# Hyena core of a two-block network: a turn-over through four banks, and the last unit's products by halves of the channels

## The chip, the cores and the metric

The kernel runs on one core of a Trainium2 chip. The metric is the device time of one execution in microseconds (us), lower being better. The program is one long kernel: a first block (delta-rule and stick-breaking mixers, gated feed-forward), a second block with an attention layer, and a third with a Hyena long convolution. The change touches only the core of the Hyena mixer, some 236 us out of about 3,126.

## The reference, cut to what matters

```python
def hyena_mixer(h, w_in, conv_w, conv_b, f_w1, ..., f_freq, skip, w_out, z, decay):
    u = dwconv3(h @ w_in, conv_w, conv_b)
    v, x1, x2 = jnp.split(u, 3, axis=-1)
    a = jnp.sin(f_freq * (z @ f_w1 + f_b1))
    a = jnp.sin(f_freq * (a @ f_w2 + f_b2))
    filt = (a @ f_w3).reshape(L, HY_ORDER, 2, D) * decay[:, None, None, :]
    ...
    k2 = k2 / jnp.sum(jnp.abs(k2), axis=0, keepdims=True)
    kf = jnp.fft.rfft(k2, axis=0)
    gates = (x1, x2)
    zc = v
    for o in range(HY_ORDER):
        zf = jnp.fft.rfft(zc, n=2 * L, axis=1)
        y = jnp.fft.irfft(zf * kf[None, :, o], n=2 * L, axis=1)[:, :L]
        zc = gates[o] * (y + skip[o] * zc)
    return zc @ w_out
```

L is 512 positions, D is 1024 channels, HY_ORDER is 2. All is float32.

## The kernel before, in words

The core works in four units, `UNITS = 2 * ORDERS`. Unit u is one order (u // 2) and one half of the channels (512 of them, u % 2). The discrete transforms are matrix products with tables of cosines and sines, split by parity of the position, so that only half the frequencies are computed and the others come from sums and differences; `f` (0 or 1) is one tile of 128 frequencies.

The steps of a unit, with names and lines of the profile:

- Turn-over, `turn_in` (L1477, TensorE): the unit's values U lie with channels on the partitions; sixteen 128x128 transposes turn them so that positions lie there, one tile t of positions per PSUM bank. The banks are `4 + t % 2`: from the third tile on TensorE waits (semaphore `y_tc`) until ScalarE has copied the bank two tiles back to ZK (`turned_in`, L1946).
- `filters` (L1439) makes the filter's values for a later unit into banks 0 to 7, pairwise, and VectorE multiplies them by the decay into PM (L2500, L2501). `filter_norm` (L1446) sums absolute values; VectorE's reciprocal rn of it (L2518) raises `y_rn`.
- `k_transform` (L1492) transforms PM into banks 0 to 3; ScalarE copies them to KS in one instruction (L1952, `y_kc`), and GpSimd forms the four sums and differences KP (L949 to L952, `y_kp`).
- `z_transform` (L1507) transforms ZK into banks 4 to 7. ScalarE copies banks 4 and 6 to XZ (L1958); VectorE's `multiply` (from L2538) makes sums and differences with banks 5 and 7 (L2538 to L2542, then `y_x`), and then the products with KP in two parts of six instructions (L2550 to L2556); each part raises `y_cb`.
- GpSimd's `y_parts` makes YF out of the products YB, two instructions behind each part (L960, L961, then L963, L964, which raises `y_y`).
- `inverse` (L1527) transforms YF back, with U's channel tile c in a bank; for the last unit the even and the odd positions of a tile go to banks of their own, `(4 + c, LAST_ODD[c])`. VectorE's `gated` scales, adds the skip term and multiplies by the gate (L2573, L2575, `y_z`). For units 2 and 3 ScalarE (L1971) and VectorE (L2564, `z_lo`) split the result into ZH and ZL, the operands of the output product `hy_out` (L490 to L492).

Each engine's instructions stand in a fixed order, written by hand, and run in that order; semaphores tie the engines. TensorE's order around the change is: for unit u, transforms of Z of u and K of u + 1, then `turn_in(u + 1)`, then `filters(u + 2)` (or, at u = 2, `z_transform(3, 0)`), then `inverse(u)`. ScalarE does `k_out(u + 1, 1)`, the KS copy, and right behind it the four copies of the turn-over. GpSimd does `y_parts(u, 0)`, `k_parts(u + 1, 0)`, `y_parts(u, 1)`, `k_parts(u + 1, 1)`. In the last unit TensorE waits for `y_x` of the whole of `multiply(3, 1)` ahead of the inverse products, because these go to banks 4 to 7, which that step reads; it then does f = 0 for all tiles and f = 1 for all tiles. The first slab of `hy_out`'s weights is split by GpSimd behind the last YF; SyncE loads the second slab once the last inverse product is done.

## Time and profile before

| what | value |
|---|---|
| median of 3 runs | 3129.38 us (3121.71 to 3134.8) |
| the profiled execution, its own time | 3128.08 us |
| its span, first to last instruction | 3125.9 us |
| TensorE (PE) busy | 2925.0 us, 94% |
| VectorE (DVE) busy | 1364.6 us, 44% |
| GpSimd (POOL) busy | 1642.2 us, 53% |
| ScalarE (ACT) busy | 714.8 us, 23% |
| mean granted clock of TensorE | 0.963 of full speed |

The profile is of one execution. A busy share is a mean over the whole program; what a change in one stage is worth is read from that stage's own timeline, where the brackets behind an instruction say how long its engine stood idle before it and who released it. A float32 product appears as two records of TensorE. Two instructions that follow one another on VectorE overlap at their ends, so the distance between two starts is less than one duration.

### The profile page before, as it was taken

What the parts mean: (1) busy time and instruction counts of PE and PEld (TensorE: products, weight loads), DVE (VectorE), ACT (ScalarE), POOL (GpSimd) and SP (SyncE); (2) the same over time, 40 slices, a digit from 0 to 9 for tenths busy, and PEclk for the clock granted to TensorE, in tenths of its full rate; (3) what the DMA queues carried; (4) which work ended last, traced back from release to release, by engine and by line L of the source; (5) the groups of instructions that cost most, each with busy time, mean ns of one, the idle gap of its engine ahead of it and who ended that gap; (6) DMA issues with size and microseconds to landing.
All of it is one profiled execution on the core that took longest, in us unless ns stands there. A gap on an engine that the chain in (4) does not pass through costs nothing.

```text
span 3125.9 us, 38862 instructions
## 1 busy us (share of the span) xinstructions
PE 2925.0 (94%) x14667; PEld 2360.3 (76%) x14667; DVE 1364.6 (44%) x1901; ACT 714.8 (23%) x1077; POOL 1642.2 (53%) x1573
## 2 busy tenths in 40 slices
PE   7997989999998999999998999999989999899998
PEld 6886888878976878788885547888867555678886
DVE  5575566321144037533334663332056677543312
ACT  2274222253243000211002562111011222121100
POOL 5652223364504666566664115667657443666663
PEclk9997899999999999999999999999999999999999
DMA  3221000022201245555652002333222110223331
GB/s 107 81 66 37 1 0 0 27 81 68 81 15 41 94 159 178 166 184 188 196 174 94 14 27 68 94 94 109 93 86 81 58 34 1 81 81 96 104 99 64
DMA packets 291816, 259.65 MB, mean 83 GB/s; under 512 B 6474, under 2 KB 264119, under 8 KB 291437
## 3 DMA queue, kind: packets, MB, share of 16 engines
q1 hardware_dynamic: 287840, 248.53, 25.5%
q0 software_dynamic: 2416, 6.57, 0.7%
q10 hardware_dynamic: 1436, 2.96, 0.3%
q8 instruction: 70, 1.15, 0.2%
q14 instruction: 54, 0.43, 0.0%
HBM read 255.94 MB, written 2.10 MB: 83 GB/s over the span
## 4 chain that ended last, share of the span: by engine, by line
PE 78%; DVE 10%; issue 5%; DVEq 2%; ACT 2%; POOL 1%; DMA 1%; POOLq 0%; ACTq 0%; SPq 0%
PE ps L490 20%; PE ps L492 20%; PE ps L491 20%; DVE cv L2045 2%; PE ps L1145 2%; PE ps L1132 1%; PE ps L1151 1%; DVE HS L627 1%; PE ps L1527 1%; PE ps L1372 1%; PE ps L1507 1%; PE ps L1362 1%; PE ps L1352 1%; PE ps L1492 1%; PE ps L1439 1%
## 5 line engine op out<-in xcount | busy, mean ns | idle before, releaser
L694 POOL CAST spl<-raw 128x512 fp32r<-128x512 f32 (+1 forms) x352 | 247.4, 703 | 730.4 <-PE ps L492 570.8
L490 PE MATMUL ps<-HSH,spl 128*128 128x512 f32 x1344 | 540.1, 402 | 40.6 <-DVE HSL L620 19.5
L696 POOL TENSOR_TENSOR spl<-raw,spl 128x512 fp32r<-128x512 f32 (+1 forms) x352 | 500.6, 1422 | 60.1 <-issue 10.5
L491 PE MATMUL ps<-HSL,spl 128*128 128x512 f32 x1344 | 529.8, 394 | 0.0
L492 PE MATMUL ps<-HSH,spl 128*128 128x512 f32 x1344 | 529.7, 394 | 0.0
L700 POOL TENSOR_TENSOR spl<-raw,spl 128x512 fp32r<-128x512 f32 (+1 forms) x352 | 480.0, 1364 | 51.5 <-issue 1.3
L490 PE MATMUL ps<-HNH,spl 128*128 128x264 f32 (+1 forms) x1152 | 370.5, 322 | 28.3 <-DVE HNL L622 6.0
L491 PE MATMUL ps<-HNL,spl 128*128 128x264 f32 (+1 forms) x1152 | 361.0, 313 | 0.0
L492 PE MATMUL ps<-HNH,spl 128*128 128x264 f32 (+1 forms) x1152 | 360.1, 313 | 0.0
L490 PEld LDWEIGHTS ps<-HSH,spl 128*128 128x128 f32 x1344 | 256.2, 191 | 121.2 <-issue 44.6
L698 POOL CAST spl<-raw 128x512 fp32r<-128x512 f32 (+1 forms) x352 | 229.6, 652 | 211.3 <-PE ps L492 209.1
L492 PEld LDWEIGHTS ps<-HSH,spl 128*128 128x128 f32 x1344 | 256.3, 191 | 54.8
L491 PEld LDWEIGHTS ps<-HSL,spl 128*128 128x128 f32 x1344 | 257.1, 191 | 52.7 <-issue 2.2
L490 PEld LDWEIGHTS ps<-HNH,spl 128*128 128x128 f32 x1152 | 222.5, 193 | 46.8 <-issue 24.2
L491 PEld LDWEIGHTS ps<-HNL,spl 128*128 128x128 f32 x1152 | 222.6, 193 | 13.2 <-issue 1.7
L492 PEld LDWEIGHTS ps<-HNH,spl 128*128 128x128 f32 x1152 | 221.4, 192 | 11.3
L490 PE MATMUL ps<-AFH,spl 128*128 128x512 f32 x528 | 208.1, 394 | 0.0
L492 PE MATMUL ps<-AFH,spl 128*128 128x512 f32 x528 | 207.2, 392 | 0.0
L491 PE MATMUL ps<-AFL,spl 128*128 128x512 f32 x528 | 205.3, 389 | 0.0
L905 POOL TENSOR_TENSOR lm<-lp,masks 128x512 f32<-128x512 f32 x56 | 74.5, 1356 | 208.3 <-DVE lp L2166 165.4
L2338 DVE TENSOR_TENSOR ps<-SG,ps 128x512 f32<-128x512 f32 x66 | 45.9, 696 | 264.6 <-PE ps L492 264.6
L2327 DVE SCALAR_TENSOR_TENSOR H<-ps,mod,H 128x512 f32<-128x512 f32 x32 | 24.0, 751 | 279.7 <-PE ps L492 279.7
(426 smaller groups left out, 4726.3 us busy)
## 6 DMA issues: line engine op xcount, KB each, us to landing
adw<-in_ada_w SPq DMA_DIRECT2D x96, 512.0 KB, 5.3
raw<-in_w_in SPq DMA_DIRECT2D x44, 1024.0 KB, 5.1
raw<-in_ffn_w_up SPq DMA_DIRECT2D x88, 512.0 KB, 4.9
raw<-in_w_ffn_in SPq DMA_DIRECT2D x44, 512.0 KB, 5.1
raw<-in_ffn_w_down SPq DMA_DIRECT2D x16, 1408.0 KB, 6.1
raw<-in_hy_w_in SPq DMA_DIRECT2D x12, 1024.0 KB, 5.1
raw<-in_w_ffn_out SPq DMA_DIRECT2D x8, 1408.0 KB, 7.0
raw<-in_w_branch_dn SPq DMA_DIRECT2D x8, 1024.0 KB, 5.1
```

Source lines behind the costliest of these rows:

```text
L490: pe.matmul(dst, w[0], x[0], start=first, stop=False)
L491: pe.matmul(dst, w[0], x[1], start=False, stop=False)
L492: return pe.matmul(dst, w[1], x[0], start=False, stop=final)
L627: dve.scalar_tensor_tensor(y_all[:, k, :], x(k), gain(k), NRS[:, 0:n], ALU.mult, ALU.mult).then_inc(n_y, 1)
L694: pool.tensor_copy(hi[:, first, :], w[:, first, :])
L696: pool.tensor_tensor(lo[:, first, :], w[:, first, :], hi[:, first, :], ALU.subtract).then_inc(split_first, 1)
L698: pool.tensor_copy(hi[:, second, :], w[:, second, :])
L700: pool.tensor_tensor(lo[:, second, :], w[:, second, :], hi[:, second, :], ALU.subtract).then_inc(split_ready, 1)
L905: pool.tensor_tensor(G["lm"][:, l % 2, :, :], G["lp"][:, 0, :, :], heads_of(masks[:, 2 + l, :], G4), ALU.mult).then_inc(E["masked"], 1)
L1145: mm = pe.matmul(ps[:, b + 2, h * P:(h + 1) * P], G["x"][:, h, :], G["lp"][:, 1, h, :], start=True, stop=True)
L2045: ins = dve.scalar_tensor_tensor(y, x[:, j:j + T], taps(j), y, ALU.mult, ALU.add)
L2338: dve.tensor_tensor(prod, SG[:, r % 2, :], ps[:, 2 * b, :], ALU.mult).then_inc(acc_free[b], 1)
```

## The change

`turn_in` writes each tile of positions to a bank of its own, 4 to 7, and no longer waits between them; ScalarE's copies read those banks. Because `filter_norm` uses bank 6 in two places, the wait for the reciprocal that reads it moves ahead of the turn-over (`y_rn` 1 ahead of `turn_in(0)`, `y_rn` 2 ahead of `turn_in(1)`), and `filters` uses banks 4 and 6 in the other order, both behind the wait for the four copies.

In the last unit `multiply(3, 1)`, VectorE's sums and products, runs over two halves of 256 channels, and so does GpSimd's `y_parts(3, 1)`. The even positions' inverse products go to banks 0 to 3 (`LAST_EVEN`), and the odd ones to 4 to 7. TensorE first does f = 0 of all even ones, then waits for `y_x` and does f = 0 of the odd ones, then f = 1 tile by tile, tiles 0 and 1 after the first half of YF, tiles 2 and 3 after the second.

```diff
-        LAST_ODD = [2 * hy_out.buf(0), 2 * hy_out.buf(1), 1, 3]
+        LAST_EVEN = [2 * hy_out.buf(0), 2 * hy_out.buf(1), 1, 3]
+        HALVES = (slice(0, SEQ // 2), slice(SEQ // 2, SEQ))
...
-            def y_parts(u, f):
+            def y_parts(u, f, x=slice(0, SEQ), done=0):
...
-                pool.wait_ge(y_cb, 4 * u + 2 * f + 1)
-                pool.tensor_tensor(YF[:, f, 0, :], c, cm, ALU.add)
+                pool.wait_ge(y_cb, 4 * u + 2 * f + 1 + done)
+                pool.tensor_tensor(YF[:, f, 0, x], c, cm, ALU.add)
...
+                    for n, x in enumerate(HALVES):
+                        y_parts(u, 1, x, 2 * n)
...
                 for t in range(NT):
-                    if t >= 2:
-                        pe.wait_ge(y_tc, u * NT + t - 1)
                     for c in range(NT):
-                        mm = pe.transpose(ps[:, 4 + t % 2, c * P:(c + 1) * P], even_odd(U[:, u % 2 * NT + c, :], t), ident)
+                        mm = pe.transpose(ps[:, 4 + t, c * P:(c + 1) * P], even_odd(U[:, u % 2 * NT + c, :], t), ident)
...
                 filter_tile(u, 0, 0)
                 filter_tile(u, 1, 2)
-                if u == 2:
-                    pe.wait_ge(y_rn, 2)
-                filter_tile(u, 2, 6)
                 pe.wait_ge(y_tc, u * NT)
-                filter_tile(u, 3, 4)
+                filter_tile(u, 2, 4)
+                filter_tile(u, 3, 6)
...
             pe.wait_ge(y_pm, NT)
+            pe.wait_ge(y_rn, 1)
             turn_in(0)
             pe.wait_ge(table_full, 32)
-            pe.wait_ge(y_rn, 1)
...
                     filter_norm(1, 6)
+                    pe.wait_ge(y_rn, 2)
                 turn_in(u + 1)
...
             z_transform(u, 1)
-            pe.wait_ge(y_x, 2 * UNITS)
             pe.wait_ge(y_z, u * NT)
-            for f in range(2):
-                pe.wait_ge(y_y, 2 * u + f + 1)
+            pe.wait_ge(y_y, 2 * u + 1)
+            for e in range(2):
+                if e:
+                    pe.wait_ge(y_x, 2 * UNITS + 1)
                 for c in range(NT):
-                    for e in range(2):
-                        mm = y_products(ps[:, (4 + c, LAST_ODD[c])[e], 0:SEQ // 2], c, e, f)
-                    if f:
-                        mm.then_inc(y_inv, 1)
+                    y_products(ps[:, (LAST_EVEN[c], 4 + c)[e], 0:SEQ // 2], c, e, 0)
+            for c in range(NT):
+                pe.wait_ge(y_y, 2 * u + 2 + c // 2)
+                for e in range(2):
+                    mm = y_products(ps[:, (LAST_EVEN[c], 4 + c)[e], 0:SEQ // 2], c, e, 1)
+                mm.then_inc(y_inv, 1)
...
-            def multiply(u, f):
+            def multiply(u, f, cols=(slice(0, SEQ),)):
                 dve.wait_ge(y_zc, 2 * u + f + 1)
                 dve.drain()
...
+                for x in cols:
+                    dve.tensor_tensor(XZ[:, 2, x], XZ[:, 0, x], ps[:, 5, x], ALU.subtract)
+                    dve.tensor_tensor(XZ[:, 3, x], ps[:, 7, x], XZ[:, 1, x], ALU.subtract)
+                    dve.drain()
+                    dve.tensor_tensor(XZ[:, 0, x], XZ[:, 0, x], ps[:, 5, x], ALU.add)
+                    dve.tensor_tensor(XZ[:, 1, x], XZ[:, 1, x], ps[:, 7, x], ALU.add).then_inc(y_x, 1)
...
+                for x in cols:
+                    zc, zs, zcm, zsm = (XZ[:, n, x] for n in range(4))
+                    kc, ks, kcm, ksm = (KP[:, f, n, x] for n in range(4))
...
-            multiply(3, 1)
+            multiply(3, 1, HALVES)
             gated(3, by_parity)
```

## Rows read from the trace of the kernel before

**Rows 1.** the page's part 4, the chain that ended last, shares by engine.

```profile
PE 78%; DVE 10%; issue 5%; DVEq 2%; ACT 2%; POOL 1%; DMA 1%; POOLq 0%; ACTq 0%; SPq 0%
```

**Rows 2.** timeline of TensorE: start, duration, line; in brackets idle before, and releaser.

```profile
2459.50 1.24 PE L1477 MATMUL ps<-square,U 128*128 128x128 f32 x8 [0.28 <-ACT ZK L1946]
...
2499.74 8.83 PE L1492 MATMUL ps<-PM,t_fwd 128*128 128x512 f32 x16 [2.42 <-DVE PM L2501]
2510.53 7.13 PE L1492 MATMUL ps<-PM,t_fwd 128*128 128x512 f32 x16 [1.97 <-ACT KS L1952]
...
2518.48 1.18 PE L1477 MATMUL ps<-square,U 128*128 128x128 f32 x8
2520.13 1.24 PE L1477 MATMUL ps<-square,U 128*128 128x128 f32 x8 [0.47 <-ACT ZK L1946]
...
2570.25 1.11 PE L1477 MATMUL ps<-square,U 128*128 128x128 f32 x8
2574.65 1.79 PE L1477 MATMUL ps<-square,U 128*128 128x128 f32 x8 [3.29 <-ACT ZK L1946]
...
2584.21 13.98 PE L1527 MATMUL ps<-t_inv,YF 128*128 128x256 f32 x64
...
2633.45 8.62 PE L1507 MATMUL ps<-ZK,t_fwd 128*128 128x512 f32 x16 [0.69 <-ACT ZK L1946]
```

**Rows 3.** timeline of ScalarE at the turn-overs of units 2 and 3.

```profile
2572.23 1.88 ACT L1952 ACTIVATE KS<-ps 128x2048 f32<-128x2048 f32 x1 [7.36 <-POOL KP L952]
...
2630.14 1.08 ACT L1946 ACTIVATE ZK<-ps 128x512 f32<-128x512 f32 x2
```

**Rows 4.** busy time by stretch; after POOL the granted clock, DMA share, GB/s.

```profile
2630.00:2633.00 3.00, 1.98 (x8) 1.58 (x8) 2.91 (x4) 2.02 (x5) 2.07 (x2) 0.50 0.01 3
```

**Rows 5.** timeline of VectorE in unit 1 and of GpSimd in unit 2.

```profile
2518.66 0.18 DVE L2518 RECIPROCAL rn<-ps 128x4 f32<-128x4 f32 x1 [1.21 <-PE ps L1446]
...
2582.07 1.28 POOL L964 TENSOR_TENSOR YF<-YB 128x512 f32<-128x512 f32 x1
```

**Rows 6.** timeline of TensorE in the last unit.

```profile
2668.62 9.82 PE L1527 MATMUL ps<-t_inv,YF 128*128 128x256 f32 x32 [5.87 <-DVE XZ L2542]
2681.30 8.62 PE L1527 MATMUL ps<-t_inv,YF 128*128 128x256 f32 x32 [2.86 <-POOL YF L964]
...
2694.46 0.50 PE L490 MATMUL ps<-ZH,spl 128*128 128x512 f32 x1 [0.40 <-DVE ZL L2564]
```

**Rows 7.** timeline of VectorE in the last unit, and of GpSimd.

```profile
2663.55 0.69 DVE L2575 TENSOR_TENSOR U<-ytmp,U 128x512 f32<-128x512 f32 x1
...
2668.73 0.69 DVE L2550 TENSOR_TENSOR YB<-XZ,KP 128x512 f32<-128x512 f32 x1 [0.16 <-issue]
...
2672.69 0.69 DVE L2550 TENSOR_TENSOR YB<-XZ,KP 128x512 f32<-128x512 f32 x1
...
2674.97 1.75 DVE L2552 TENSOR_TENSOR YB<-XZ,KP 128x512 f32<-128x512 f32 x1
...
2678.01 0.68 DVE L2556 TENSOR_TENSOR YB<-YB,YT 128x512 f32<-128x512 f32 x1
2684.85 0.88 DVE L2573 SCALAR_TENSOR_TENSOR ytmp<-ps,rn,ytmp 128x256 f32<-128x256 f32 x2 [6.16 <-PE ps L1527]
...
2693.72 1.47 DVE L2564 TENSOR_TENSOR ZL<-U,ZH 128x512 fp32r<-128x512 f32 x2
...
2679.99 1.26 POOL L964 TENSOR_TENSOR YF<-YB 128x512 f32<-128x512 f32 x1
```

**Rows 8.** groups by form: line, shapes, count, busy us, mean ns, idle before.

```profile
L2573 DVE SCALAR_TENSOR_TENSOR ytmp<-ps,rn,ytmp 128x512 f32<-128x512 f32 x12 | 9.0, 748 | 9.4 <-PE ps L1527 9.3 <-issue 0.2
...
L2573 DVE SCALAR_TENSOR_TENSOR ytmp<-ps,rn,ytmp 128x256 f32<-128x256 f32 x8 | 3.5, 476 | 6.2 <-PE ps L1527 6.2
...
L696 POOL TENSOR_TENSOR spl<-raw,spl 128x512 fp32r<-128x512 f32 x304 | 411.9, 1355 | 53.2 <-issue 10.5
...
L696 POOL TENSOR_TENSOR spl<-raw,spl 128x768 fp32r<-128x768 f32 x48 | 88.7, 1848 | 6.9
```

More of the change, by code:

```diff
@@ L952, in k_parts @@
                 pool.tensor_tensor(KP[:, f, 3, :], so, se, ALU.subtract).then_inc(y_kp, 1)
-            def y_parts(u, f):
+            def y_parts(u, f, x=slice(0, SEQ), done=0):
                 if u:
                     pool.wait_ge(y_inv, u * NT)
-                c, si, cm, sm = (YB[:, n, :] for n in range(4))
-                pool.wait_ge(y_cb, 4 * u + 2 * f + 1)
-                pool.tensor_tensor(YF[:, f, 0, :], c, cm, ALU.add)
-                pool.tensor_tensor(YF[:, f, 2, :], c, cm, ALU.subtract)
-                pool.wait_ge(y_cb, 4 * u + 2 * f + 2)
-                pool.tensor_tensor(YF[:, f, 1, :], si, sm, ALU.subtract)
-                pool.tensor_tensor(YF[:, f, 3, :], si, sm, ALU.add).then_inc(y_y, 1)
+                c, si, cm, sm = (YB[:, n, x] for n in range(4))
+                pool.wait_ge(y_cb, 4 * u + 2 * f + 1 + done)
+                pool.tensor_tensor(YF[:, f, 0, x], c, cm, ALU.add)
+                pool.tensor_tensor(YF[:, f, 2, x], c, cm, ALU.subtract)
+                pool.wait_ge(y_cb, 4 * u + 2 * f + 2 + done)
+                pool.tensor_tensor(YF[:, f, 1, x], si, sm, ALU.subtract)
+                pool.tensor_tensor(YF[:, f, 3, x], si, sm, ALU.add).then_inc(y_y, 1)
             filter_in(0)
@@ L2533, in _ @@
                         norm_out(0, 6)
-            def multiply(u, f):
+            def multiply(u, f, cols=(slice(0, SEQ),)):
                 dve.wait_ge(y_zc, 2 * u + f + 1)
                 dve.drain()
-                dve.tensor_tensor(XZ[:, 2, :], XZ[:, 0, :], ps[:, 5, :], ALU.subtract)
-                dve.tensor_tensor(XZ[:, 3, :], ps[:, 7, :], XZ[:, 1, :], ALU.subtract)
-                dve.drain()
-                dve.tensor_tensor(XZ[:, 0, :], XZ[:, 0, :], ps[:, 5, :], ALU.add)
-                dve.tensor_tensor(XZ[:, 1, :], XZ[:, 1, :], ps[:, 7, :], ALU.add).then_inc(y_x, 1)
+                for x in cols:
[4 more added lines that the diff above has]
+                    dve.tensor_tensor(XZ[:, 1, x], XZ[:, 1, x], ps[:, 7, x], ALU.add).then_inc(y_x, 1)
                 dve.drain()
@@ L2546, in multiply @@
                     dve.wait_ge(y_y, 2 * u + f)
-                zc, zs, zcm, zsm = (XZ[:, n, :] for n in range(4))
-                kc, ks, kcm, ksm = (KP[:, f, n, :] for n in range(4))
-                for part, (a, b, am, bm), op in ((0, (kc, ks, kcm, ksm), ALU.subtract), (1, (ks, kc, ksm, kcm), ALU.add)):
-                    dve.tensor_tensor(YB[:, part, :], zc, a, ALU.mult)
-                    dve.tensor_tensor(YT[:, 0, :], zs, b, ALU.mult)
-                    dve.tensor_tensor(YB[:, 2 + part, :], zcm, am, ALU.mult)
-                    dve.tensor_tensor(YT[:, 1, :], zsm, bm, ALU.mult)
-                    dve.drain()
-                    dve.tensor_tensor(YB[:, part, :], YB[:, part, :], YT[:, 0, :], op)
-                    dve.tensor_tensor(YB[:, 2 + part, :], YB[:, 2 + part, :], YT[:, 1, :], op).then_inc(y_cb, 1)
-                    dve.drain()
+                for x in cols:
+                    zc, zs, zcm, zsm = (XZ[:, n, x] for n in range(4))
+                    kc, ks, kcm, ksm = (KP[:, f, n, x] for n in range(4))
+                    for part, (a, b, am, bm), op in ((0, (kc, ks, kcm, ksm), ALU.subtract), (1, (ks, kc, ksm, kcm), ALU.add)):
+                        dve.tensor_tensor(YB[:, part, x], zc, a, ALU.mult)
+                        dve.tensor_tensor(YT[:, 0, x], zs, b, ALU.mult)
+                        dve.tensor_tensor(YB[:, 2 + part, x], zcm, am, ALU.mult)
+                        dve.tensor_tensor(YT[:, 1, x], zsm, bm, ALU.mult)
+                        dve.drain()
+                        dve.tensor_tensor(YB[:, part, x], YB[:, part, x], YT[:, 0, x], op)
+                        dve.tensor_tensor(YB[:, 2 + part, x], YB[:, 2 + part, x], YT[:, 1, x], op).then_inc(y_cb, 1)
+                        dve.drain()
             pairs = lambda x: x.rearrange("p (t e) -> p t e", e=2)
@@ L2583, in _ @@
             whole = lambda b, y: [(split(ps[:, b, :]).rearrange("p e t -> p t e"), y)]
-            by_parity = lambda c, y: [(ps[:, (4 + c, LAST_ODD[c])[e], 0:SEQ // 2], y[:, :, e]) for e in range(2)]
+            by_parity = lambda c, y: [(ps[:, (LAST_EVEN[c], 4 + c)[e], 0:SEQ // 2], y[:, :, e]) for e in range(2)]
             multiply(0, 0)
@@ L2596, in _ @@
             norm_out(1, 6)
-            for t, b in enumerate((0, 2, 6, 4)):
+            for t, b in enumerate((0, 2, 4, 6)):
                 filter_out(2, t, b)
@@ L2602, in _ @@
             multiply(1, 1)
-            for t, b in enumerate((0, 2, 6, 4)):
+            for t, b in enumerate((0, 2, 4, 6)):
                 filter_out(3, t, b)
```

5 lines of the change are left out of this document (3 added, 2 removed).

## The prediction

> **What bounds the kernel now.** I read the page first: the chain of waits, followed back from the end, lies 78% on TensorE's matmuls and only 10% on VectorE [rows 1]. So a change elsewhere pays only where TensorE stands still. Next I read TensorE's timeline through the Hyena core, about 2458 to 2696 us of a span of 3125.9 us, and looked only at the idle figure in brackets behind each stretch [rows 2, 6]. It shows two kinds of place. At the turn-overs (L1477) TensorE stops after the second bank until ScalarE has emptied the first: 0.28, 0.47 and 3.29 us in units 0 to 2, and 3.29 us again in unit 3 (to 2630.78; its row repeats unit 2's). At the last unit it waits 5.87 us for VectorE's sums (XZ) and 2.86 us for GpSimd's YF. Then I read ScalarE at the two long stops [rows 3]: its copy of the turned bank sits behind the copy KS, and KS itself waited for GpSimd (7.36 us). Last came VectorE and GpSimd in the last unit and the widths of their instructions [rows 7, 8].
>
> TensorE's clock matters, because both edits only move its pauses. The window right after the 3.29 us stop has a granted clock of 0.50, the 1.2 GHz level [rows 4]. In durations: sixteen 512-column records cost 7.13 us after a pause of 1.97 us, but 8.83 us after 2.42 us [rows 2] (a second pause of 1.97 us, up to 2483.31, was free as well), and 32 of 256 columns cost 9.82 us after 5.87 us and 8.62 us after 2.86 us [rows 6], where a full-clock row of 64 costs 13.98 us, so 6.99 us for 32 [rows 2]. So a pause of up to 1.97 us was free here, and pauses from 2.42 us up cost another 1.6 to 2.8 us in the next stretch.
>
> **Turn-over, units 0 and 1.** Nothing is added on TensorE: the same 16 transpose records per unit, 8 taking 1.11 us, so about 0.134 us each and 2.15 us in all. Unit 0 loses its stop of 0.28 us; the moved wait (y_rn 1) is set in VectorE's order before the last two tiles of hy_in, so it costs nothing. Gain 0.28. In unit 1 a stop of 0.47 us goes [rows 2], but TensorE now waits for y_rn 2 ahead of the transposes: the reciprocal ran 2518.66 to 2518.84 [rows 5], and the transposes had started at 2518.48 [rows 2], so 0.4 us is added. Behind that wait on TensorE stand the transposes, the filters and the inverse. Net between -0.3 and +0.5, I take +0.1.
>
> **Turn-over, unit 2.** Before: transposes to 2571.36, stop, the rest from 2574.65, filters behind them, inverse(1) at 2584.21 [rows 2]. After: the transposes end at 2572.4; the filters want banks 0 to 3, hence KS, which ends at 2574.11 [rows 3]; they start at 2574.2 after 1.75 us of idling, which is under 1.97 and so keeps the clock, and their 16 records take 6.9 us, to 2581.1. But inverse(1) needs GpSimd's last YF, which ends at 2583.35 [rows 5]. Nothing in the change moves that one: its chain runs through VectorE's products and GpSimd's KP, not through the turn-over. So at most 0.8 us (2584.21 less 2583.4) is won, and TensorE stands 2.3 us in front of the inverse. That is between the free 1.97 and the dear 2.42, nearer to the second: I take it that the clock falls, and 1.7 us comes on top. Net -0.9 us, a loss (ends: +0.8 if the clock holds, -2.0 with the dearest restart). z(2,0) stands right behind on TensorE, so this passes on.
>
> **Turn-over, unit 3.** z(3,0) wants all four copies. Before, it started at 2633.45 [rows 2]. After, all four banks are full when KS ends, and the copies run at a cadence of 0.49 us from 2630.14 (two in 1.08 us, [rows 3]): 2630.14 + 3 x 0.49 + 0.6 = 2632.2. So z(3,0) starts at 2632.3 instead of 2633.45, 1.15 us sooner. Its pause is now one piece of 3.7 us, and the clock falls as before; z(3,0) cost 8.62 us against 7.03, 1.6 more. A fresh restart may cost 1.6 to 2.8. I take 1.8: gain 1.0 (ends 0 and 1.3).
>
> **Last unit.** The halves first make work. A 128x512 scalar_tensor_tensor lasts 0.748 us, a 128x256 one 0.476 us [rows 8], so half the columns saves 0.27 of it. The same off the tensor_tensor (0.68, issued every 0.605 us) gives 0.42 us, every 0.335 us. XZ then takes 8 instructions instead of 4, +0.42 us; a product part (6 instructions, two drains) goes from 3.96 us (2668.73 to 2672.69, [rows 7]) to 2 x 2.32 us, +0.68, and there are two parts, +1.36. On GpSimd the 512- and 768-column rows, 1355 and 1848 ns [rows 8], give about 2 ns a column; half of a YF instruction (1.26 us, [rows 7]) then takes 0.70 us.
>
> VectorE and GpSimd hinder each other: next to a YF instruction a product took 1.75 us instead of 0.68, and two of them were hit, 2.1 us in all [rows 7]. With halves, three of the four GpSimd pairs lie beside products instead of one of two. At about 0.55 us lost per half instruction that is 6 x 0.55 = 3.3 us against 2.1. So VectorE's last product ends 0.42 + 1.36 + 1.2 = 3.0 us later, at 2681.8 instead of 2678.69, and the last YF, two half instructions, at 2683.5 instead of 2681.25. This edit makes the last operand later; it wins because half of the f = 1 work no longer waits for it.
>
> TensorE after: the even products of f = 0 start when U of the last tile is done, 2664.3 [rows 7], 16 records, 3.45 us. The odd ones wait for the ninth y_x, about 2669.05, to 2672.5. YF's first half is ready at 2676.9: the first half of the first part is due at 2671.4, the second part and two contended pairs follow. Sixteen records at the low clock and then the high one end at about 2682. The last sixteen run from 2683.5 to 2687.0, after a pause of 1.5 us, at full clock. Before, hy_out began at 2689.57. Next late is ZL: gating starts at 2682.0 instead of 2684.85 and took 10.34 us to the last ZL at 2695.19 (tile 0 of hy_out waited 0.40 us for one, [rows 6]). The hy_out splits of GpSimd start 2.2 us later and so lie longer beside it; I add 1 us: 2693.3 against 2695.19, and tile 0's end, a microsecond behind, comes 1.9 us sooner; without that extra, 2.8. I take 2.3 (ends -2.0, below, and +3.5). SyncE's load of the second hy_out slab waits for the last inverse, which comes sooner; its data was first needed 4 us after it landed.
>
> The Trainium skill (VectorE: DVE Perf Modes, "The TRN2 errata — SBUF-src ops pay a fixed extra latency per instruction") says that the bubble is paid per instruction and advises tiles of at least 512 elements, which speaks against halves. Its formula (N + 151)/0.96 makes 424 ns of one, and the sum stays as it is. The same skill (SBUF — State Buffer, "Who interferes with whom") says that a VectorE instruction with two SBUF inputs and a GpSimd one that reads SBUF exclude each other for the whole instruction. The rows of before show 1.07 us lost per 1.23 us of GpSimd. Taken strictly, six half instructions would cost 0.15 us more each, an estimate by that page, and the gain of the last unit would be 1.4 us.
>
> **Sum.** 0.28 + 0.1 - 0.9 + 1.0 + 2.3 = 2.8 us saved. The rest of the kernel behind is TensorE-bound, so it passes through. The profiled execution took 3128.08 us (span 3125.9 and 2.2 around it): 3125.3. The median of the three runs is 1.3 us above it and gives 3126.6; I say 3126. What a measurement here can tell from no change is about 0.5%, 16 us.
>
> **Rivals.** (A) The forecast, 3126, chance 0.42. (B) The clock holds in front of inverse(1), +1.7, and the contention scales better than I took it, to the upper end of the last unit, +1.2: 5.7 us saved, 3123. For it: 2.3 us is a near thing, and two pauses of 1.97 us were free. Against it: 2.42 us was not. Chance 0.28. (C) Slower: a contended instruction costs the same whatever its width. Place: the last unit, while GpSimd's YF lies beside VectorE's products. Price: the three pairs would cost 2 x (1.68 - 0.335) = 2.7 us each, 8.1 instead of 3.3, so +4.8 us; YF would end at 2689.2 after 2.46 us for the last pair, the last products at 2692.7, tile 0 of hy_out at 2698.2, 2.0 us later than before. It decides once a half GpSimd instruction costs over about 1.0 us. With the turn-overs (+0.5) that is 1.5 us slower: 3130 to 3131. For it: the extra instructions are certain. Against it: GpSimd's rows fall with width. Chance 0.15. (D) The change does not do what it says: the four banks take away TensorE's stop but the copy KS and GpSimd's YF stay the late ones, and restarts at the low clock eat the turn-overs (-2.0, 0 in unit 3), leaving the last unit's 2.3 less 1.6: 0.7 saved, 3128. Chance 0.15.
>
> All of these lie within 0.5%. The three runs of before spread over 13 us, more than any of my terms, so the range is mostly theirs: 3117 to 3134. Faster by over 0.5% would need 16 us where all the pauses that the change touches hold 0.28 + 0.47 + 3.29 + 3.29 + 5.87 + 2.86 = 16 us: 0.03. Slower by over 0.5%: 0.02. Within: 0.95.
>
> **What would show it.** Right: no pause inside L1477; a pause of about 1.8 us in front of L1439 and of 2.3 us in front of inverse(1), with a granted clock under 1 behind it; z(3,0) 1.1 us closer to KS; in the last unit 256-column products of 0.42 us and GpSimd ones of 0.7; hy_out's first matmul about 2.5 us sooner after z(3,1). Wrong: inverse(1) at once at full clock (B), half-width instructions over 1.2 us beside GpSimd (C), or a span that differs by over 10 us.

## The result, and the profile after

| | before | after |
|---|---|---|
| median of 22 runs each | 3126.32 us (3120.65 to 3134.8) | 3131.35 us (3124.74 to 3136.27) |
| profiled execution, its own time | 3128.08 us | 3133.04 us |
| mean granted clock | 0.963 | 0.964 |

The ratio after/before is 1.0015 [1.0008, 1.0021]: the changed kernel is 4.7 us (2.5 to 6.6) slower. The forecast was 2.8 us saved. That is within 0.5%, and 3131 us lies between the 3117 and 3134 stated, but the forecast had the sign wrong.

The page's first line and its part 4 (the chain that ended last, shares by engine) hardly differ from [rows 1]; a loss of 5 us cannot be seen there.

```profile
span 3131.2 us, 38888 instructions
...
PE 78%; DVE 10%; issue 5%; DVEq 3%; ACT 2%; POOL 1%; DMA 1%; POOLq 0%; ACTq 0%; SPq 0%
```

It can in TensorE's timeline (start, duration, line; in brackets idle before, and releaser). The first seven rows answer to units 0 and 1 of [rows 2], the rest to units 2 and 3; line numbers have moved: L1479 turn-over, L1443 filters, L1494 and L1509 the transforms of K and Z, L1450 filter_norm, L1527 inverse.

```profile
2458.79 2.07 PE L1479 MATMUL ps<-square,U 128*128 128x128 f32 x16
...
2483.43 5.41 PE L1443 MATMUL ps<-W,A 128*128 128x512 f32 x8 [1.97 <-ACT KS L1956]
...
2500.52 7.13 PE L1494 MATMUL ps<-PM,t_fwd 128*128 128x512 f32 x16 [1.38 <-DVE PM L2505]
2509.62 8.83 PE L1494 MATMUL ps<-PM,t_fwd 128*128 128x512 f32 x16 [1.97 <-ACT KS L1956]
2521.22 1.83 PE L1450 MATMUL ps<-ones,AS 128*128 128x1 f32 x8 [2.77 <-DVE AS L2517]
2523.32 3.69 PE L1479 MATMUL ps<-square,U 128*128 128x128 f32 x16 [0.28 <-DVE rn L2522]
2526.80 7.66 PE L1443 MATMUL ps<-W,A 128*128 128x512 f32 x16
...
2576.47 2.07 PE L1479 MATMUL ps<-square,U 128*128 128x128 f32 x16
2580.37 7.14 PE L1443 MATMUL ps<-W,A 128*128 128x512 f32 x16 [1.83 <-ACT KS L1956]
2589.62 14.08 PE L1527 MATMUL ps<-t_inv,YF 128*128 128x256 f32 x64 [2.10 <-POOL YF L965]
...
2631.89 2.07 PE L1479 MATMUL ps<-square,U 128*128 128x128 f32 x16
2637.76 8.58 PE L1509 MATMUL ps<-ZK,t_fwd 128*128 128x512 f32 x16 [3.79 <-ACT ZK L1950]
```

Positions are best counted from the start of the first K transform: 2460.70 in this trace, 2460.58 before. K(1,0) and K(1,1) stand for the two K transforms of unit 1, f = 0 and f = 1, and filters(1,0) for the eight filter records at 2483.43. What the reader is to see, step by step:

- Turn-over of unit 0: one piece of 2.07 us, no stop inside. From its start to the first K transform it is 1.91 us; before, 2.47 [rows 2].
- Filters at 2483.43, behind a pause of 1.97 us: eight records in 5.41 us. The same pause cost nothing before (3.71 us at 2483.31). So the next pause shrinks from 2.42 to 1.38 us, and K(1,0), sixteen records, runs at full clock: 7.13 us instead of 8.83 [rows 2]. It ends at 46.95 instead of 47.99.
- Yet filter_norm starts at 60.52 and had started at 57.01: TensorE stands 2.77 us for VectorE's sum AS. Then 0.28 us for the reciprocal, and the clock has fallen: transposes 3.69 us, filters 7.66 us.
- Turn-over of unit 2: no stop inside (2.07 us), 1.83 us ahead of the filters, 2.10 us ahead of inverse(1), which takes 14.08 us, full clock.
- Turn-over of unit 3: one pause of 3.79 us, z(3,0) 8.58 us.

Busy time by stretch of the same kernel (after POOL the granted clock): 0.62 in K(1,1) and 0.54 from the norm on, full speed in inverse(1), where [rows 4] had 0.50 behind the stop.

```profile
2510.00:2514.00 4.00, 4.00 (x7) 1.73 (x6) 3.91 (x3) 0.00 (x0) 4.00 (x3) 0.62 0.00 0
2521.00:2524.00 3.00, 2.51 (x11) 2.45 (x12) 0.26 (x2) 0.00 (x0) 3.00 (x3) 0.54 0.02 5
2590.00:2594.00 4.00, 4.00 (x20) 3.54 (x19) 2.60 (x5) 0.00 (x0) 4.00 (x4) 1.00 0.00 0
```

Unit 1 is where the time went. VectorE and GpSimd of after (the answer to VectorE's row in [rows 5]), L2561 and L2562 being the last two products of multiply(0,1), L2515 and L2517 the filter sums, L950 and L951 the differences KP:

```profile
2509.89 1.60 DVE L2561 TENSOR_TENSOR YB<-YB,YT 128x512 f32<-128x512 f32 x1
2511.41 1.74 DVE L2562 TENSOR_TENSOR YB<-YB,YT 128x512 f32<-128x512 f32 x1
2513.25 1.58 DVE L2515 TENSOR_TENSOR AB<-AB 128x512 f32<-128x512 f32 x1
...
2519.47 1.60 DVE L2517 TENSOR_TENSOR AS<-AS,AB 128x512 f32<-128x512 f32 x1
2523.08 0.18 DVE L2522 RECIPROCAL rn<-ps 128x4 f32<-128x4 f32 x1 [2.01 <-PE ps L1450]
...
2509.66 1.29 POOL L950 TENSOR_TENSOR KP<-KS 128x512 f32<-128x512 f32 x1 [7.07 <-ACT KS L1956]
2510.90 1.71 POOL L951 TENSOR_TENSOR KP<-KS 128x512 f32<-128x512 f32 x1
```

And the same place before:

```profile
2509.72 0.68 DVE L2556 TENSOR_TENSOR YB<-YB,YT 128x512 f32<-128x512 f32 x1
2510.50 0.69 DVE L2511 TENSOR_TENSOR AB<-AB 128x512 f32<-128x512 f32 x1
2511.27 1.60 DVE L2513 TENSOR_TENSOR AS<-AS,AB 128x512 f32<-128x512 f32 x1
...
2510.57 1.75 POOL L949 TENSOR_TENSOR KP<-KS 128x512 f32<-128x512 f32 x1 [8.78 <-ACT KS L1952]
```

After, KP starts at 2509.66, ahead of the two last products: they take 1.60 and 1.74 us, and each filter sum behind them 1.6 to 1.7. Before, the products were over at 2510.40 and KP began at 2510.57, so that only the sums were met. That accounts for the whole delay: multiply(0,1) runs 0.66 us later, its last two products take 1.97 us more and the first sum 0.89 us more (the other three are met in both, 1.60 to 1.72 us), together 3.5 us, and the norm starts 3.5 us later.

ScalarE at the turn-overs of units 2 and 3 (answer to [rows 3]): the last ZK copy now ends 3.83 us after the start of KS (2633.87 to 2637.70); before, the last of four ended at 2633.40, 5.04 us after KS started at 2628.36.

```profile
2578.44 1.88 ACT L1956 ACTIVATE KS<-ps 128x2048 f32<-128x2048 f32 x1 [7.36 <-POOL KP L953]
...
2635.64 2.06 ACT L1950 ACTIVATE ZK<-ps 128x512 f32<-128x512 f32 x4
```

Last unit, TensorE (answer to [rows 6]) and then VectorE and GpSimd (answer to [rows 7]). L2557 is a product, L2579 and L2581 gating, L2570 ZL, L961 and L964 YF, L694 the first split of hy_out.

```profile
2668.57 3.72 PE L1527 MATMUL ps<-t_inv,YF 128*128 128x256 f32 x16 [1.56 <-DVE U L2581]
2673.32 3.72 PE L1527 MATMUL ps<-t_inv,YF 128*128 128x256 f32 x16 [1.02 <-DVE XZ L2547]
2680.82 5.41 PE L1527 MATMUL ps<-t_inv,YF 128*128 128x256 f32 x16 [3.78 <-POOL YF L965]
2687.51 3.72 PE L1527 MATMUL ps<-t_inv,YF 128*128 128x256 f32 x16 [1.29 <-POOL YF L965]
2690.88 0.59 PE L490 MATMUL ps<-ZH,spl 128*128 128x512 f32 x1
...
2698.70 0.80 PE L490 MATMUL ps<-ZH,spl 128*128 128x512 f32 x1 [2.95 <-DVE ZL L2570]
```

```profile
2675.78 0.43 DVE L2556 TENSOR_TENSOR YB<-XZ,KP 128x256 f32<-128x256 f32 x1
2676.12 0.95 DVE L2557 TENSOR_TENSOR YT<-XZ,KP 128x256 f32<-128x256 f32 x1
...
2686.13 0.88 DVE L2579 SCALAR_TENSOR_TENSOR ytmp<-ps,rn,ytmp 128x256 f32<-128x256 f32 x2 [0.16 <-issue]
...
2689.48 1.76 DVE L2570 TENSOR_TENSOR ZL<-U,ZH 128x512 fp32r<-128x512 f32 x1
...
2692.10 1.60 DVE L2581 TENSOR_TENSOR U<-ytmp,U 128x512 f32<-128x512 f32 x1
...
2696.90 2.76 DVE L2570 TENSOR_TENSOR ZL<-U,ZH 128x512 fp32r<-128x512 f32 x2
...
2675.83 0.95 POOL L961 TENSOR_TENSOR YF<-YB 128x256 f32<-128x256 f32 x1 [9.29 <-DVE YB L2562]
...
2679.18 0.72 POOL L964 TENSOR_TENSOR YF<-YB 128x256 f32<-128x256 f32 x1 [1.53 <-DVE YB L2562]
...
2687.40 1.08 POOL L694 CAST spl<-raw 128x512 fp32r<-128x512 f32 x1
```

A product of half the width takes 0.43 us alone and 0.95 beside GpSimd; GpSimd's half takes 0.72 alone and 0.95 beside VectorE. hy_out's first matmul comes at 2690.88. Shifted by the 4.27 us by which this unit starts later, before's (2689.57) would be 2693.84, so it is 2.96 us sooner. But gating, 2686.13 to 2699.66, takes 13.53 us where it took 10.34 [rows 7]: a ZL of 1.76, a U of 1.60, two ZL in 2.76. TensorE stops 2.95 us for a ZL at 2698.70 and restarts at the low clock (0.80 us). GpSimd's side shows where the time went. Before, its first eight splits ran from 2681.20 to 2691.10 and it then stood 4.26 us for the load of the second slab, so VectorE gated alone for the last 4.1 us:

```profile
2695.36 0.61 POOL L694 CAST spl<-raw 128x512 fp32r<-128x512 f32 x1 [4.26 <-DMA raw<-in_hy_w_out]
```

After, the eight run from 2687.40 to 2698.10, beside nearly all of the gating.

By steps, after less before: turn_in(0) -0.56; first K transform to inverse(0) 73.60 less 67.49, +6.1; inverse(0) to inverse(1) 55.32 less 56.14, -0.8; to inverse(2) 56.55 less 57.70, -1.15; inverse(2) to VectorE's second addition into H 61.30 less 59.84, +1.5. Sum +5.0; the spans differ by 5.3.

### The profile page after: what moved, and what is told of

It is laid out like the page before. It is cut to its first block, busy times and chain, and to the rows that moved or that the text cites. A ratio compares the mean times of both kernels' runs of the same rounds, so it can differ in the third digit from the quotient of the medians.

```text
span 3131.2 us, 38888 instructions
## 1 busy us (share of the span) xinstructions
PE 2926.7 (93%) x14667; PEld 2361.1 (75%) x14667; DVE 1372.8 (44%) x1917; ACT 714.4 (23%) x1077; POOL 1648.1 (53%) x1577
## 3 DMA queue, kind: packets, MB, share of 16 engines
q10 hardware_dynamic: 1436, 2.96, 0.3%
q8 instruction: 70, 1.15, 0.2%
## 4 chain that ended last, share of the span: by engine, by line
PE 78%; DVE 10%; issue 5%; DVEq 3%; ACT 2%; POOL 1%; DMA 1%; POOLq 0%; ACTq 0%; SPq 0%
PE ps L490 20%; PE ps L492 20%; PE ps L491 20%; DVE cv L2049 2%; PE ps L1149 2%; PE ps L1136 2%; PE ps L1509 1%; PE ps L1155 1%; PE ps L1376 1%; PE ps L1366 1%; DVE HS L627 1%; PE ps L1527 1%; PE ps L1356 1%; DVE HSL L620 1%; PE ps L1443 1%
## 5 line engine op out<-in xcount | busy, mean ns | idle before, releaser
L694 POOL CAST spl<-raw 128x512 fp32r<-128x512 f32 (+1 forms) x352 | 248.6, 706 | 725.4 <-PE ps L492 569.2
```

The source lines that it names most:

```text
L694: pool.tensor_copy(hi[:, first, :], w[:, first, :])
```

## The experiments

Each kernel was profiled once and, but for two, timed against before in five rounds. What the traces gave is in one table; a label is explained below it. Columns: duration of filters(1,0), K(1,0) and K(1,1); start of filter_norm and of inverse(0), both counted from the first K transform; inverse(0) to inverse(2); inverse(2) to the second addition into H; median (before's on the same chip); ratio.

| kernel | filters(1,0) | K(1,0) | K(1,1) | norm | inv(0) | inv(0)-inv(2) | last unit | median (before) | ratio [95%] |
|---|---|---|---|---|---|---|---|---|---|
| before | 3.71 | 8.83 | 7.13 | 57.01 | 67.49 | 113.84 | 59.84 | | |
| before_again | 3.71 | 8.83 | 7.13 | 56.99 | 67.48 | 113.86 | 59.88 | 3127.48 (3128.91) | 0.9989 [0.9979, 0.9999] |
| before_third | 3.71 | 8.83 | 7.13 | 57.00 | 67.50 | 113.89 | 59.88 | 3127.18 (3127.06) | 1.0002 [0.9991, 1.0012] |
| after | 5.41 | 7.13 | 8.83 | 60.52 | 73.60 | 111.87 | 61.30 | 3131.35 (3126.32) | 1.0015 [1.0008, 1.0021] |
| after_again | 3.71 | 8.83 | 8.83 | 58.62 | 68.74 | 112.16 | 61.57 | 3129.82 (3128.91) | 1.0008 [0.9998, 1.0017] |
| after_third | 5.40 | 7.13 | 8.83 | 60.53 | 73.54 | 111.84 | 61.28 | 3130.26 (3126.92) | 1.0006 [0.9996, 1.0016] |
| turn_only | 3.71 | 7.13 | 8.83 | 59.85 | 71.61 | 111.87 | 59.86 | 3131.10 (3128.91) | 1.0005 [0.9996, 1.0014] |
| halves_only | 5.41 | 7.13 | 7.13 | 60.53 | 71.80 | 114.24 | 61.32 | 3129.68 (3128.91) | 1.0001 [0.9992, 1.0010] |
| after_wait | 3.71 | 7.13 | 8.83 | 58.12 | 68.32 | 113.52 | 61.62 | 3128.79 (3127.41) | 1.0003 [0.9994, 1.0012] |
| turn_wait | 5.41 | 7.13 | 8.83 | 58.78 | 70.49 | 113.39 | 59.85 | 3130.19 (3127.41) | 1.0001 [0.9992, 1.0010] |
| order_only | 5.41 | 7.13 | 8.83 | 60.52 | 73.56 | 111.86 | 59.82 | 3131.77, one run | |
| gemm_held | 5.41 | 7.13 | 7.13 | 60.52 | 73.61 | 113.80 | | 3138.97, one run | |
| late_turn | 5.41 | 7.13 | 7.13 | 60.51 | 71.78 | 113.23 | 59.83 | 3124.59 (3127.06) | 0.9992 [0.9983, 1.0001] |
| late_turn_wait | 3.71 | 8.83 | 7.13 | 56.99 | 67.48 | 112.88 | 59.83 | 3125.16 (3127.06) | 0.9994 [0.9985, 1.0003] |
| rn_between | 5.41 | 7.13 | 8.83 | 60.53 | 73.38 | 114.54 | 59.84 | 3133.07 (3127.06) | 1.0016 [1.0007, 1.0025] |
| sums_after | 3.71 | 7.13 | 8.83 | 56.93 | 69.21 | 113.10 | 61.63 | 3130.22 (3126.92) | 1.0004 [0.9995, 1.0013] |
| sums_before | 5.41 | 7.13 | 7.13 | 55.89 | 66.45 | 112.93 | 59.93 | 3127.06 (3126.92) | 0.9994 [0.9985, 1.0003] |
| sums_turn | 5.40 | 7.13 | 8.83 | 57.59 | 68.91 | 115.00 | 59.84 | 3127.80 (3126.92) | 1.0002 [0.9993, 1.0011] |
| sums_late | 3.71 | 8.83 | 7.13 | 56.93 | 67.51 | 112.99 | 59.85 | 3127.11 (3128.90) | 0.9987 [0.9978, 0.9996] |
| sums_late_halves | 3.71 | 8.83 | 7.13 | 56.94 | 67.51 | 112.90 | 61.63 | 3127.37 (3128.90) | 0.9994 [0.9985, 1.0003] |

The kernel before, timed against itself, gave 0.9989 [0.9979, 0.9999]: an interval here can be off by about 0.1%. Times tell little between neighbours in this table; the reasons rest on the traces, each of one execution.

**Which edit, and does it repeat.** turn_only is before with the four banks; halves_only is after with the old turn-over (two banks, old waits and filter banks). before_again and after_again are the two kernels unchanged.

```diff
-                        mm = pe.transpose(ps[:, 4 + t, ...
+                        mm = pe.transpose(ps[:, 4 + t % 2, ...
```

> The four-bank turn-over and its moved waits alone; the last unit is as before. Theory L (the halves lose): the turn-over wins 2 us in units 2 and 3 (0.8 and 1.2, as in the profile after) and the loss of 5.5 us up to inverse(0) in that profile was a chance of the clock: the time is 0 to 2 us under the kernel before. Theory T (the turn-over loses): the wait for the reciprocal in front of turn_in(1), behind a later filter_norm, costs 4 to 6 us up to inverse(0) in every run, and the time is 2 to 4 us above before. In the profile: from the start of the first K transform to inverse(0), 67.5 us in the trace before and 73.6 in the one after; L says nearer 68, T nearer 73.

> The last unit by halves alone; the turn-over is as before. Theory L: the gating of the last unit lies wholly beside GpSimd's weight splits and takes 13.5 us instead of 10.3, TensorE waits for ZL in the first tile of hy_out and loses its clock there: from z(3,1)'s start to the first H of hy_out 141.7 in place of 140.5 would be the wrong base, so in steps: start of z(3,1) to the first addition into H was 40.5 us before and 41.7 after, and L expects 41.7 again, with the time 1 to 3 us above before. Theory T: the last unit is a gain or nothing, the time is that of before or up to 1 us under it.

> The changed kernel once more, for the spread of its clock falls. If the 5.5 us lost up to inverse(0) are the change's own, this profile shows them again (first K transform to inverse(0) near 73.6 us); if they are chance, it may show anything from 67 to 74. Time near 1.0015 of before either way.

> The kernel before once more. The time is its own within 0.1%. The step from the first K transform to inverse(0) was 67.5 us in its trace; if chance decides there, another value between 67 and 74 is as likely, if not, 67.5 again.

The last unit's 1.5 us go with the halves (59.86 without, 61.32 with). The late norm does not go with either edit: halves_only, with the old turn-over, has it too, and after_again, with both edits, has K(1,0) at 8.83 us and the norm at 58.62 (there KP came behind the products, but K(1,1) took 8.83 us instead of before's 7.13, and the norm follows it at once). So identical code runs in more than one way, and the four banks can only be a push towards one.

**A wait against the collision; the cost of gating.** after_wait and turn_wait make GpSimd's first KP of unit 1 wait for the end of multiply(0,1). gemm_held makes GpSimd's splits wait for the end of gating; order_only is after with TensorE's new order and banks but one slice of 512 columns.

```diff
+                if u == 0:
+                    pool.wait_ge(y_cb, 4)          # after_wait, turn_wait
                 if u + 1 < UNITS:
                     k_parts(u + 1, 0)
...
+            pool.wait_ge(y_z, UNITS * NT)          # gemm_held
             for gm in (hy_out, fc_in[1], fc_out[1]):
...
-        HALVES = (slice(0, SEQ // 2), slice(SEQ // 2, SEQ))
+        HALVES = (slice(0, SEQ),)                  # order_only
```

> The changed kernel, with one wait more on GpSimd: k_parts(1,0) starts only when multiply(0,1) is done (y_cb 4). Theory C (collision): in unit 1 GpSimd's KP instructions meet the tail of VectorE's products whenever TensorE ran K(1,0) at full clock, and the filter sums and filter_norm come 2 to 4 us later for it (filter_norm 56.99 and 57.01 us after the first K transform without the meeting, 59.9 to 60.5 with it). With the wait filter_norm comes by 57.5 in any state, inverse(0) by 68.5, and the median falls 1 to 4 us. Rival R (the wait costs what it saves): GpSimd is the late one anyway, KP(1,0) and with it KS(1,1) come later, filter_norm stays at 58 to 60.5 and the time does not change.

> The four-bank turn-over alone, last unit as before, with the same wait on GpSimd in unit 1. If the parts add (turn-over -2.5 us, last unit by halves +1.5 us, collision 0 to +6 us by chance), this is the sum of the good ones: inverse(0) by 68 us after the first K transform, units 2 and 3 together 1.9 us shorter than before, the last unit 54.4 us from inverse(2) to the first addition into H, and a time 2 to 5 us under before. If the collision is not the cause, the time is that of turn_only, 1.0005 of before.

> The changed kernel with GpSimd's splits of hy_out's weights held back until the last gating is done (y_z 16). Made to read one thing: the gating with no GpSimd beside it. Theory S (shared access): from its first instruction to the last ZL the gating took 10.3 us before and 13.5 after, where the splits lay beside all of it; alone it takes 7 to 8.5 us. Rival: it is bound by TensorE's last products and by ScalarE's copies, and stays above 10 us. The time of the whole kernel is 2 to 6 us more, for hy_out's first tile now waits for its weights.

> The changed kernel with one slice of 512 channels instead of two halves: TensorE's new order of the last unit (even products first, banks 0 to 3) stays, VectorE and GpSimd work at full width. Inverse(2) to the first addition into H took 54.4 us before and 55.2 after, and the second addition came at 59.9 and 61.3. If the halves cost and the order is free, this gives 54.0 to 54.6 and 59.5 to 60.1; if the order itself costs (its pauses lose the clock in front of f = 1), 55 and 61 as after.

after_wait is to be compared with turn_only and turn_wait with after, each pair having the same durations of filters(1,0), K(1,0) and K(1,1). With the wait the norm starts at 58.12 instead of 59.85 and at 58.78 instead of 60.52, inverse(0) 3.3 and 3.1 us sooner: part of the loss, since the sums are still met. Both times missed what I had expected: turn_wait, 2 to 5 us under before, came out at 1.0001, and after_wait's norm was to be there by 57.5. (One of turn_wait's 11 runs took 9354.93 us; the median leaves it aside.) VectorE in gemm_held, gating alone, and then in order_only:

```profile
2687.47 0.88 DVE L2580 SCALAR_TENSOR_TENSOR ytmp<-ps,rn,ytmp 128x256 f32<-128x256 f32 x2 [0.16 <-issue]
...
2690.82 0.69 DVE L2571 TENSOR_TENSOR ZL<-U,ZH 128x512 fp32r<-128x512 f32 x1
...
2695.50 1.70 DVE L2571 TENSOR_TENSOR ZL<-U,ZH 128x512 fp32r<-128x512 f32 x2
```

```profile
2688.52 0.88 DVE L2579 SCALAR_TENSOR_TENSOR ytmp<-ps,rn,ytmp 128x256 f32<-128x256 f32 x2 [6.12 <-PE ps L1527]
...
2697.42 1.47 DVE L2570 TENSOR_TENSOR ZL<-U,ZH 128x512 fp32r<-128x512 f32 x2
```

Gating alone takes 9.73 us (2687.47 to 2697.20), its ZL 0.69 us. I had expected 7 to 8.5, which missed, because before's 10.34 holds only 0.6 of contention; but 13.53 against 9.73 is 3.8 us lost to the splits. Holding the splits back costs more than it saves. In order_only gating starts 3.6 us behind the first split, as before (3.65; in after it starts 1.3 us ahead of it), and takes 10.37 us (2688.52 to 2698.89), and the last unit 59.82, as before: the new order is free, and the halves cost all of it.

The Trainium skill (SBUF — State Buffer, "Who interferes with whom") calls it an exclusive lock on a shared port pair. The rows nearly agree, with neither engine shut out for long: 0.69 became 1.76 us on VectorE and 1.27 became 1.71 on GpSimd. Side by side each starts an instruction about every 1.67 us (VectorE before, 2673.30 to 2674.97; GpSimd in turn_only, 2509.63 to 2511.30), where alone they do so every 0.61 and 1.23 us; strict turns would make 1.84, an estimate from these two.

**Four banks only where TensorE stood long.** late_turn uses four banks in units 2 and 3 and the old last unit; late_turn_wait adds the wait above; rn_between is turn_only with the wait for `y_rn` 2 between banks 5 and 6.

```diff
-                    if t >= 2:
+                    if t >= 2 and u < 2:           # late_turn
...
+                    if u == 1 and t == 2:
+                        pe.wait_ge(y_rn, 2)        # rn_between
```

> The kernel before with four banks for the turn-overs of units 2 and 3 only; units 0 and 1 and the last unit as before. Both theories expect 1.9 us out of units 2 and 3 (inverse(0) to inverse(1) 55.3 for 56.1, inverse(1) to inverse(2) 56.6 to 57 for 57.7). Theory O (the changed code in units 0 and 1 meets the late state more often): here that stretch is before's, filter_norm at 57.0 and inverse(0) at 67.5 is likelier than not, and the time is 0.5 to 3 us under before. Theory N (the state of that stretch is chance with any code): 57 or 60.5 equally, the time moves by noise only, within 1.5 us of before.

> The same with GpSimd's k_parts(1,0) behind the end of multiply(0,1). The wait took filter_norm from 59.9 to 60.5 down to 58.1 to 58.8 where K(1,0) ran at full clock; where it ran at the low one it should do nothing (57.0). Expected: filter_norm 57.0 to 58.8, inverse(0) under 70, a time 1 to 4 us under before; the best of the versions if the parts add.

> turn_only with the wait for the reciprocal (y_rn 2) between the second and the third bank, the first that needs it (bank 6). Theory: the wait in front cost 0.28 us of standing plus its part of a low clock; the step from filter_norm to the filters was 3.61 us before at full clock, 3.25 after at full clock, 5.58 after and 4.40 in halves_only at the low one. With the wait between the banks it is 3.2 to 3.3 at full clock and 4.3 to 4.5 at the low one. Rival: the third bank waits as long as the first did and nothing changes (3.25, or 4.3 to 5.6). Time within 2 us of turn_only.

> The kernel before a third time, for the state of the stretch up to inverse(0) and for what identical kernels differ by. Theory O: filter_norm at 57.0, inverse(0) at 67.5 again. Theory N: either. Time: 0.999 to 1.001.

late_turn has K(1,0) quick and the norm late with before's own code up to there. What the moved wait costs is seen between kernels whose norm ran at the same clock. With a norm of 1.02 us (full clock) inverse(0) follows 11.27 us behind the norm's start in halves_only and late_turn, without the moved wait, and 11.76 in turn_only, with it. With a norm of 1.7 to 1.8 us (low clock) it is 13.0 to 13.1 in after, gemm_held and order_only and 12.85 in rn_between. So once the norm is late, the moved wait costs 0.2 to 0.5 us and saves nothing; the rest, 1.3 us and more, is whether the clock had already fallen when the norm began. rn_between's inverse(1) took 15.77 us: there the clock fell, as the forecast had it.

**Take the sums out of the collision.** If the norm is late because the filter sums and the last products meet KP, the sums done ahead of multiply(0,1) must give an early norm although K(1,0) runs at full clock. If the quick K(1,0) or the clock is itself the price, they must not.

```diff
+            filter_abs(1, 3)                       # ScalarE, ahead of k_out(1, 0)
...
-            multiply(0, 1)
             filter_sum(1, 2)
             filter_sum(1, 3)
+            multiply(0, 1)
```

sums_after and sums_before are this edit on after and on before, sums_turn on before with four banks everywhere and rn_between's wait.

> The changed kernel with the filter sums of unit 1 (tiles 2 and 3) in front of multiply(0,1) on VectorE, and ScalarE's filter_abs(1,3) in front of its KS copy. Theory C (collision): filter_norm(1) has its sums early and never waits; it comes by 57.5 us after the first K transform in any state, at 55.3 where both K transforms run at full clock, inverse(0) by 68.5; the time falls by 3 to 5 us from the changed kernel's, to 0.999 to 1.000 of before. Rival: the products, pushed back by 4 us, make KP and KS(1,1) late instead; filter_norm stays at 58 or later and the time at 1.001.

> The kernel before with the same move. If it is mostly in the good state (67.5 us to inverse(0) in three of three traces), the move gives little: 0 to 1.5 us, time 0.9995 to 1. If half its executions are in the late state, 2 us or more: 0.999 to 0.9995. In the trace inverse(0) comes by 67.5 in any state.

> Four banks at every turn-over with the reciprocal's wait between banks 5 and 6, the last unit as before, and the early sums. The sum of the parts: 0.56 in unit 0, 1 to 2 us in units 2 and 3, no late state, no halves: 2 to 5 us under before, 0.9985 to 0.9993. If the changed turn-over loses by itself in unit 1, it stays at 1.000 to 1.001.

> The changed kernel a third time. Its two traces gave 73.6 and 68.7 us from the first K transform to inverse(0); kernels with the same code there gave 71.6, 73.6, 73.6 and 73.4. If the late state goes with the code, 71 or more is likely here (about 5 in 6); if it is chance with any code, as likely under 69.

TensorE, then VectorE, in sums_before (L1492 K, L1446 norm, L2512 filter sum, L2554 and L2555 the products that KP meets):

```profile
2497.45 7.13 PE L1492 MATMUL ps<-PM,t_fwd 128*128 128x512 f32 x16 [1.38 <-DVE PM L2500]
...
2513.52 0.95 PE L1446 MATMUL ps<-ones,AS 128*128 128x1 f32 x8
...
2500.71 0.69 DVE L2512 TENSOR_TENSOR AS<-AS,AB 128x512 f32<-128x512 f32 x1
...
2506.94 1.60 DVE L2554 TENSOR_TENSOR YB<-YB,YT 128x512 f32<-128x512 f32 x1
2508.46 1.75 DVE L2555 TENSOR_TENSOR YB<-YB,YT 128x512 f32<-128x512 f32 x1
```

K(1,0) is quick (7.13) and KP still meets the products (1.60 and 1.75 us), yet the sums are done by 2501.4 and the norm starts at 55.89, inverse(0) at 66.45, the earliest of all kernels, where halves_only and late_turn with the same quick K(1,0) had 71.8. The move alone could be suspected, since it takes the sums out from behind the products whether these are met or not. But in halves_only the two products and four sums take 9.85 us where 4.1 would do alone, 5.7 us more, and TensorE stood 4.48 us for them: by these rows it would not have stood at all without the collision. And the wait above, which spares only the two products, brought the norm 1.7 us forward. Together that shows the collision as the cause of the late norm. The time of sums_before cannot be told from before's all the same (0.9994 [0.9985, 1.0003]). In sums_after the norm is early too (56.93), but TensorE then waits 2.44 us for the reciprocal, which now stands behind multiply(0,1) on VectorE: the moved `y_rn` wait again, which the old turn-over asks for only later. inverse(0) comes at 69.21, over the 68.5 that I had expected. sums_turn stands 1.40 us for it between the banks, has inverse(0) at 68.91 and then loses the clock in inverse(1) (15.77 us): 1.0002, where I had expected 2 to 5 us under before.

**What the parts suggest together.** sums_late is late_turn with the early sums; sums_late_halves adds the halves of the last unit.

> The kernel before with four banks in the turn-overs of units 2 and 3 only, and the early filter sums in unit 1. If the parts add: inverse(0) 66.4 to 67.5 us after the first K transform in any state, inverse(0) to inverse(2) 112 to 113.5 for 113.9, the last unit 54.35 from inverse(2) to the first addition into H; 2 to 4 us under before, 0.9985 to 0.9995, and under both kernels. If not (the gain goes to the clock again), 0.9995 to 1.0005.

> The same with the last unit by halves of the channels, as in the change. Theory: the gating beside the weight splits costs 1.5 us by the second addition into H (61.3 to 61.6 after inverse(2) for 59.85), with nothing else moved: the time is 1 to 2 us over sums_late's. Rival: the cost belonged to the late state and its phase, and is gone here (59.9).

```profile
2495.05 8.83 PE L1492 MATMUL ps<-PM,t_fwd 128*128 128x512 f32 x16 [2.43 <-DVE PM L2502]
...
2512.81 0.95 PE L1446 MATMUL ps<-ones,AS 128*128 128x1 f32 x8
```

TensorE in sums_late: K(1,0) at the low clock here, norm at 56.93, so its early sums were not put to the test in this trace. 0.9987 [0.9978, 0.9996] is the lowest ratio of all, some 4 us under before, though the two medians are only 1.8 us apart. The interval ends where the lowest of after's three begins, and before itself once gave 0.9989: it is likely better than after, and not shown to be better than before. The halves on top cost 1.8 us in the trace.

## Why the prediction was wrong, step by step

**What bounds the kernel.** Held: only TensorE's pauses paid or cost. But the inference "a pause of up to 1.97 us was free here" was wrong. It came from two rows. Over the 20 traces here the clock was low behind a pause of 1.97 us in 10 of 20 cases at filters(1,0) and in 10 of 20 at K(1,1).

**Turn-over, units 0 and 1: the step that failed.** Unit 0: 0.56 gained for 0.28. Unit 1: "Net between -0.3 and +0.5, I take +0.1"; it lost 6.1. I counted the stop removed and the wait added on TensorE, and took VectorE's sums to be where they had been. Two things were missing. First, this unit has two pauses at which the clock may fall, and executions of the same code differ in which. Where it holds ahead of filters(1,0), K(1,0) starts behind a pause of 2.4 us, and was slow in 7 of those 10 traces; where it falls there, the pause is 1.38 us, and K(1,0) was at full clock in 10 of 10. Second, a quick K(1,0) brings KP forward by 1 us while slow filters put multiply(0,1) back by 0.65, and they meet: the norm comes 3.5 us late, with the clock lost on the way. A faster stretch of TensorE made the kernel slower. On top of it the moved `y_rn` wait costs 0.2 to 0.5 us in that case; the forecast's 0.4 for it was about right, and nearly all of the 6.1 us came from what it had put at nothing.

How often it happens decides the sum. K(1,0) was slow, the good case, in 6 of 9 traces with the old turn-over in unit 0 and in 1 of 11 with four banks. K(1,1) shows it more clearly: behind the same 1.97 us pause it took 8.83 us in 10 of the 11 traces with the changed turn-over in unit 0 (banks, wait and order of the filter banks together), and 7.13 us in all 9 with the old one. That costs 1.7 us even without the collision (after_again's norm at 58.62). So the clock's falls are not chance alone: they go with the code, and the changed turn-over brings more of them. Why is open. TensorE does the same work from there on, and nothing I varied shows how a 0.56 us shorter turn-over, 23 us and more earlier, would act. Leaving out the kernels with the extra wait or the early sums, the mean to inverse(0) is 72.6 over seven traces with four banks and 69.2 over five without: +3.4 us.

**Turn-over, unit 2.** "Net -0.9", the clock falling ahead of inverse(1), with +0.8 if it holds. The pauses came as worked out (1.83 for 1.75, 2.10 for 2.3), but the clock held in after: +0.8. It fell in 3 of the 10 traces with a 2.1 us pause there (gemm_held, rn_between, sums_turn: inverse(1) 15.7 to 15.8). In the other 5 of the 15 four-bank traces it had fallen already behind the pause of 1.83 to 1.86 us (filters of unit 3 8.8 us instead of 7.14), which the forecast had called safe, and inverse(1) then waited 0.4 us only. inverse(1) started 0.8 us sooner in all 15.

**Turn-over, unit 3.** 1.0 forecast, 1.15 measured, with one pause of 3.79 us (3.7 forecast) and z(3,0) at 8.58. That agreement holds for after's traces (0.9 to 1.2 us gained in the three), and not beyond: over all four-bank traces z(3,0) took 8.5 to 10.2 us, and the step from inverse(1) to inverse(2), with the slow inverse(1) in it, was 57.7 us with four banks (15) and without (5). Both units together: 113.0 us with, 113.75 without, so 0.75 gained on average.

**Last unit.** Most terms stood: halves of 0.42 us, 0.95 beside GpSimd (I took 0.9), the last product at 2685.97 (2681.8 + 4.27 = 2686.1), the last YF at 2687.45 (2687.8), hy_out 2.96 us sooner (about 2.5). (Half of a YF was put at 0.70 us, though 1.26 less 256 columns at 2 ns is 0.75; 0.72 was measured.) The mis-sized term is "I add 1 us" for gating beside the splits: 13.53 instead of 10.34, so 3.2. The sentence that the second slab was "first needed 4 us after it landed" had a row the wrong way round: GpSimd waited 4.26 us for it, and that gap is part of why gating met so little contention before. With it comes TensorE's wait of 2.95 us and a restart at the low clock. 2.3 us of gain became 1.5 us of loss; over seven traces with halves 61.5 us, over twelve without 59.85, so +1.6.

**The sum.** 3.4 - 0.56 - 0.75 + 1.6 = 3.7 us slower on average (after's three traces less before's three give 3.5), beside 4.7 (2.5 to 6.6) measured and 2.5 and 1.9 in the two repeats.

**The rivals.** B was right of inverse(1) in after, and of nothing else. C had the sign, but its mechanism is refuted: a contended half took 0.95 us, a whole one 1.75 [rows 7]. D missed for after, where the stops went and both late turn-overs gained; over all four-bank traces its "0 in unit 3" came true. Most of the loss came from a place that none of them named, unit 1; the last unit's share came from the gating, which C did not name either.
